# The linear half of an expert's first bias taken off TensorE: ScalarE copies the product out, GpSimd adds the bias

## What is computed

```python
def expert_block(args):
    xblk, e = args                      # 128 rows of one expert
    hh = xblk @ w1[e] + b1[e]           # 1024 -> 2048
    glu = jnp.minimum(hh[:, :D_FF], SWIGLU_LIMIT)
    lin = jnp.clip(hh[:, D_FF:], -SWIGLU_LIMIT, SWIGLU_LIMIT)
    act = glu * jax.nn.sigmoid(SWIGLU_ALPHA * glu) * (lin + 1.0)
    return act @ w2[e] + b2[e]
```

## Time and profile before

| | us |
|---|---|
| median of three runs | 2271.59 (2271.05 to 2272.78) |
| the profiled execution | 2271.8 |
| its span, first to last instruction | 2269.9 |
| TensorE busy in the span | 2235.8 |
| VectorE, ScalarE, GpSimd busy | 1768.0, 1238.6, 429.3 |
| start of item 0 to end of the last | about 1087 to 2260 |

### The profile page before, as it was taken

One profiled execution on the slowest core, in us unless ns is written; L12 is line 12 of the kernel. 1 busy time (PEld: TensorE's weight loads), 2 busy tenths in 40 slices (PEclk: granted clock), 3 DMA queues, 4 the chain that ended last, 5 costly groups with the idle time before them and its releaser, 6 DMA issues.

```text
span 2269.9 us, 30685 instructions
## 1 busy us (share of the span) xinstructions
PE 2235.8 (98%) x10681; PEld 1828.9 (81%) x10681; DVE 1768.0 (78%) x1652; ACT 1238.6 (55%) x1154; POOL 429.3 (19%) x421
## 2 busy tenths in 40 slices
PE   7999999999999999999999999999999999999998
PEld 3888888888887887888788888888888888888886
DVE  6756655555646766757899999999999999999997
ACT  6322132222225624632777777777777777777774
POOL 3000000000221132102522222222212222223222
PEclk9999999999999999999999999999999999999999
DMA  8322223131321121146899999999999999999995
GB/s 301 121 93 93 98 88 130 56 130 57 105 98 38 38 75 38 57 149 215 310 360 367 374 373 375 386 367 371 381 362 372 370 369 383 370 376 372 385 365 199
DMA packets 135516, 542.98 MB, mean 239 GB/s; under 512 B 16131, under 2 KB 24467, under 8 KB 101390
## 3 DMA queue, kind: packets, MB, share of 16 engines
q1 hardware_dynamic: 123192, 516.30, 60.1%
q0 software_dynamic: 11952, 21.44, 3.9%
q10 hardware_dynamic: 296, 4.21, 0.5%
HBM read 533.79 MB, written 26.38 MB: 247 GB/s over the span
## 4 chain that ended last, share of the span: by engine, by line
PE 95%; DMA 2%; DVE 1%; POOL 1%; ACT 0%; issue 0%; SPq 0%; POOLq 0%; DVEq 0%
PE ps L2272 90%; PE ps L2828 1%; PE ps L2840 1%; PE ps L2619 1%; POOL list_d L865 1%; DMA ar<-h_d,ar 0%; DMA ar<-in_ctx 0%; PE ps L2564 0%; DMA out_x<-ar,cur 0%; DMA raw<-in_w_mod 0%; PE ps L2510 0%; PE ps L2384 0%; DVE nmx L1875 0%; ACT hhi L1026 0%; PE ps L2717 0%
## 5 line engine op out<-in xcount | busy, mean ns | idle before, releaser
L2272 PE MATMUL ps<-whi,yhi 128*128 128x512 f32 x1072 | 346.5, 393 | 0.1
L2272 PE MATMUL ps<-hhi,yhi 128*128 128x512 f32 x1072 | 342.6, 389 | 0.0
L2092 DVE TENSOR_TENSOR hlo<-raw,hhi 128x2048 fp32r<-128x2048 f32 x132 | 302.6, 2294 | 47.3 <-ACT hhi L1333 47.3
L1333 ACT ACTIVATE whi<-raw 128x2048 fp32r<-128x2048 f32 x132 | 253.5, 1921 | 98.9 <-PE ps L2272 98.9
L2092 DVE TENSOR_TENSOR wlo<-raw,whi 128x2048 fp32r<-128x2048 f32 x132 | 298.7, 2282 | 3.4 <-ACT whi L1333 1.9
L1333 ACT ACTIVATE hhi<-raw 128x2048 fp32r<-128x2048 f32 x132 | 253.1, 1918 | 76.5 <-PE ps L2272 76.5
L1450 DVE TENSOR_TENSOR wlo<-raw,whi 128x2048 fp32r<-128x2048 f32 x56 | 128.2, 2289 | 159.5 <-ACT whi L995 159.4
L2272 PEld LDWEIGHTS ps<-whi,yhi 128*128 128x128 f32 x1072 | 201.2, 188 | 53.9 <-issue 12.1
L2272 PEld LDWEIGHTS ps<-hhi,yhi 128*128 128x128 f32 x1072 | 201.2, 188 | 41.7
L2272 PE MATMUL ps<-whi,hhi 128*128 128x512 f32 x592 | 233.3, 394 | 0.0
L2272 PE MATMUL ps<-whi,hlo 128*128 128x512 f32 x592 | 230.8, 390 | 0.0
(11 more groups left out here) (355 smaller groups left out, 4436.6 us busy)
## 6 DMA issues: line engine op xcount, KB each, us to landing
raw<-in_exp_w SPq DMA_DIRECT2D x264, 1024.0 KB, 7.7
ar<-in_exp_w SPq DMA_DIRECT2D x132, 1024.0 KB, 7.6
raw<-in_w_in SPq DMA_DIRECT2D x44, 1024.0 KB, 5.0
raw<-in_w_mod SPq DMA_DIRECT2D x22, 1024.0 KB, 6.4
raw<-in_w_br_ret SPq DMA_DIRECT2D x8, 1024.0 KB, 5.0
ar<-in_x SPq DMA_DIRECT2D x8, 512.0 KB, 7.4
raw<-in_w_br_diff SPq DMA_DIRECT2D x4, 1024.0 KB, 5.1
raw<-in_w_out SPq DMA_DIRECT2D x4, 1024.0 KB, 9.6
```

Of the source, the lines that this page charges most:

```text
L1333: act.activation(e_whi[j % ESPL], e_raw[s], ACT.Copy).then_inc(e_hi, 1)
L2092: V.tensor_tensor(e_wlo[j % ESPL], e_raw[s], e_whi[j % ESPL].bitcast(F32), ALU.subtract).then_inc(e_lo, 1)
L2272: return pe.matmul(out, lhsT, rhs, start=start, stop=stop, skip_group_check=skip)
```

## The change

- TensorE adds the bias of the gated half alone: two matmuls for four. The table `bias` shrinks to 512 columns with the gated half's first 512 columns in rows 0 to 63 and its second 512 in rows 64 to 127; banks 4 and 5 now begin with their first product.
- Before the stage, ScalarE adds the 1 to the linear half of b1 and stores it (two DMAs from its own queue) in a scratch tensor in DRAM, `acc_d`.
- SP loads, for each item, the row of its expert from there, broadcast to 128 partitions (128 x 1024, `load_linear_bias`, into `A_LIN`), between the loads of w1 and w2.
- ScalarE copies the linear half out of PSUM (`linear_out`) into `A_AC`; it makes the last chunk's high part before it and takes the Silu only after `x_high`.
- GpSimd adds `A_LIN` to `A_AC` (`add_linear_bias`). For this its order changes: column, add and gather stand ahead of the wait for the landing.
- VectorE clips in place in SBUF, after the last chunk's split and `x_low`.

```diff
-        bias = [hh[0][:, 2, q, :] for q in range(2)]
+        bias = hh[0][:, 2, 0, :]
...
+            def load_linear_bias(e, i):
+
+                if not isinstance(i, int):
+                    sp.wait_ge(moe_step, i * 3)
+                sp.dma_start(F(A_LIN, D), acc_d[one(e), :].broadcast_to((P, D))).then_inc(b_loaded, 16)
...
+            sp.wait_ge(stored, 16 * (LT + 2))
+            load_linear_bias(0, 0)
             with sp.Fori(1, N_EXPERTS) as i:
                 for j in range(FIRST):
                     load_w1(i, i, j)
+                load_linear_bias(i, i)
                 for k in range(MOE_N - FIRST):
                     load_w2(i - 1, i, FIRST + k, k)
...
+            def add_linear_bias(i):
+
+                pool.wait_ge(b_loaded, i * 16 + 16 * (BIASES + 1))
+                pool.wait_ge(moe_step, i * 3 + 1)
+                hold()
+                pool.tensor_tensor(out=F(A_AC, D), in0=F(A_AC, D), in1=F(A_LIN, D), op=ALU.add).then_inc(moe_step, 1)
...
+                next_sel(i, e1)
+                add_linear_bias(i)
+                next_gather(i, code2, i * 4 + 1)
                 if not isinstance(k, int) or k:
                     take_rows(k)
-                next_sel(i, e1)
-                next_gather(i, code2, i * 4 + 1)
+                    pool.wait_ge(cur_ready, k + 1)
+                    hold()
...
             next_sel(0, 1)
+            add_linear_bias(0)
             next_gather(0, 2, 1)
...
+            def linear_out(i):
+                act.wait_ge(e_used, chunk(i, FIRST - 1) + 1)
+                act.activation(F(A_AC, D), psf[:, 4 * COL:6 * COL], ACT.Copy).then_inc(moe_step, 1)
...
+                hi_e(i, MOE_N - 1)
+                linear_out(i)
+                x_high(i + 1)
                 glu(i)
-                hi_e(i, MOE_N - 1)
-                x_high(i + 1)
...
+            act.activation(linear, linear, ACT.Identity, bias=ones[0:2 * N_EXPERTS, 0:1]).then_inc(bias_hi, 1)
+            act.activation(bias, F(A_BSRC, COL), ACT.Copy).then_inc(bias_hi, 1)
             act.wait_ge(bias_hi, 1)
-            for q in range(2):
-                act.activation(bias[q], bsrc[:, q * COL:(q + 1) * COL], ACT.Copy).then_inc(bias_hi, 1)
+            for r in range(2):
+                act.dma_start(acc_d[0:N_EXPERTS, r * COL:(r + 1) * COL],
+                              linear[32 * r:32 * r + 32, :]).then_inc(stored, 16)
...
-            def activate(i, between):
-
-                dve.wait_ge(e_used, chunk(i, FIRST - 1) + 1)
-                V.tensor_scalar(ac, psf[:, 4 * COL:6 * COL], 1.0 - LIMIT, 1.0 + LIMIT, ALU.max,
-                                ALU.min).then_inc(moe_step, 1)
-                between()
+            def activate(i):
+
+                dve.wait_ge(moe_step, i * 3 + 2)
+                V.tensor_scalar(ac, ac, 1.0 - LIMIT, 1.0 + LIMIT, ALU.max, ALU.min).then_inc(moe_step, 1)
                 dve.wait_ge(glu_done, i + 1)
-                dve.wait_ge(moe_step, i + 1)
+                dve.wait_ge(moe_step, i * 3 + 3)
...
-                activate(i, lambda: lo_e(i, MOE_N - 1))
+                lo_e(i, MOE_N - 1)
                 x_low(i + 1)
+                activate(i)
...
-                    for b in (0, 2, 1, 3):
-                        r = slice(b // 2 * 64, b // 2 * 64 + 64)
-                        last = mm(ps[:, 2 + b, :], sel[r, :], bias[b % 2][r], not late, False)
+                    for b in range(2):
+                        r = slice(b * 64, b * 64 + 64)
+                        last = mm(ps[:, 2 + b, :], sel[r, :], bias[r], not late, False)
...
-                        mm(o, xthi[:, kk, :], wh, late and kk == 0, False)
+                        mm(o, xthi[:, kk, :], wh, kk == 0 and (late or b > 1), False)
```

More of the change, by code:

```diff
@@ L137 @@
 A_XG, A_Y, A_GS, A_TH, A_AC = 0, 1024, 2048, 3072, 9216
+A_LIN, A_LSRC = A_TH, A_BSRC + COL
+BIASES = 6
 MOD_A = 2 * D // COL
@@ L696, in _ @@
             for r in range(4):
-                sp.dma_start(F(A_BSRC, D)[32 * r:32 * r + 32, :], a["exp_b1"][:, r // 2 * D:(r // 2 + 1) * D]).then_inc(b_loaded, 16)
+                sp.dma_start(F(A_BSRC, COL)[32 * r:32 * r + 32, :],
+                             a["exp_b1"][:, r // 2 * COL:(r // 2 + 1) * COL]).then_inc(b_loaded, 16)
+            for r in range(2):
+                sp.dma_start(F(A_LSRC, COL)[32 * r:32 * r + 32, :],
+                             a["exp_b1"][:, D + r * COL:D + (r + 1) * COL]).then_inc(b_loaded, 16)
             def one(e):
@@ L749, in extra @@
                     load_w1(e, i, j)
+                load_linear_bias(e, i)
                 for k in range(MOE_N - FIRST):
@@ L762, in _ @@
             sp.wait_ge(last_added, 32)
-            sp.wait_ge(stored, 16 * LT)
+            sp.wait_ge(stored, 16 * (LT + 2))
         @block.gpsimd
@@ L956, in _ @@
             next_sel(0, 1)
+            add_linear_bias(0)
             next_gather(0, 2, 1)
             pool.sem_inc(pool_m, 3)
-            pool.wait_ge(stored, 16 * LT)
+            pool.wait_ge(stored, 16 * (LT + 2))
             for t in range(LT):
@@ L1385, in _ @@
             hi_e(0, 1)
-            act.wait_ge(b_loaded, 64)
-            bsrc = F(A_BSRC, D)
-            act.activation(bsrc[64:128, :], bsrc[64:128, :], ACT.Identity, bias=ones[64:128, 0:1]).then_inc(bias_hi, 1)
+            act.wait_ge(b_loaded, 16 * BIASES)
+            linear = F(A_LSRC, COL)[0:2 * N_EXPERTS, :]
+            act.activation(linear, linear, ACT.Identity, bias=ones[0:2 * N_EXPERTS, 0:1]).then_inc(bias_hi, 1)
+            act.activation(bias, F(A_BSRC, COL), ACT.Copy).then_inc(bias_hi, 1)
             act.wait_ge(bias_hi, 1)
-            for q in range(2):
-                act.activation(bias[q], bsrc[:, q * COL:(q + 1) * COL], ACT.Copy).then_inc(bias_hi, 1)
+            for r in range(2):
+                act.dma_start(acc_d[0:N_EXPERTS, r * COL:(r + 1) * COL],
+                              linear[32 * r:32 * r + 32, :]).then_inc(stored, 16)
             hi_e(0, 2)
@@ L1403, in bias_out @@
                 if t == 0:
-                    act.wait_ge(stored, 16 * LT)
+                    act.wait_ge(stored, 16 * (LT + 2))
                 act.wait_ge(gb_done, t + 1)
@@ L1418, in _ @@
             act.activation(junk32[:, 0:1], ones[:, 0:1], ACT.Silu)
+            linear_out(0)
             glu(0)
@@ L2227, in _ @@
             dve.wait_ge(ones_made, 5)
[L2228 to L2232, removed]
+            dve.wait_ge(bias_hi, 2)
+            V.scalar_tensor_tensor(out=bias, in0=bias.bitcast(F32), scalar=low_rows[:, 0:1],
+                                   in1=F(A_BSRC, COL), op0=ALU.mult, op1=ALU.add).then_inc(bias_lo, 1)
             dve.wait_ge(gb_hi, 2)
@@ L2241, in _ @@
                 lo_e(1, j)
-            activate(0, lambda: None)
+            activate(0)
             x_low(1)
@@ L2861, in up @@
                         pe.wait_ge(xt_lo, 2)
-                        pe.wait_ge(bias_lo, 2)
+                        pe.wait_ge(bias_lo, 1)
                         add_bias()
```

## The result

The changed kernel takes **2284.66 us** (median; 2283.33 to 2286.35), the kernel before 2271.65 (2271.05 to 2272.78) in the same runs: ratio 1.0059, 95% interval 1.0047 to 1.0070. It is 13.0 us slower, outside the range of the forecast. Its profiled execution took 2283.33 us, span 2281.5.

A forecast was written before the change was run, and what follows sets the result against it. TensorE was taken as the bound, busy for 98% of the span. Terms of -7.4 us (bias matmuls) and +4.8 us (start), the others 0, summed to -2.6 us: 2269.0 us predicted, range for 8 in 10 from 2264 to 2282.

The forecast's parts named there:

- The pair of bias matmuls: TensorE, each item: two bias matmuls fewer save 0.23 us, over 32 items -7.4 us (-4.8 to -10.7).
- The longer chain: Behind each item, through ScalarE, GpSimd's add and VectorE's clip: next split 0.9 us later, within spare time, 0 us.
- The third rival: Small stalls in some items, about 0.3 us on average, turn -2.6 into +7: 2279 us; chance 0.08.
- More DMA: One more 0.52 MB broadcast per item, queued on SP between w1 and w2, fits the DMA stream: 0 us.
- Rival 1: Broadcast has no room in the DMA stream: 1.40 us per item, +48 us, 2320; full form or part, chance 0.11.
- The start: Start of expert stage: item 0's add, queued behind GpSimd's list wait, delays item 1's bias matmuls, +4.8 us (+3.5 to +7).

The follow-up runs named there:

- the small load: The changed kernel, but after item 0 the transfer of the linear bias carries 32 of its 1,024 columns, GpSimd still adding all 1,024: 2275.2 us.

## Why the prediction was wrong, point by point

- **The pair of bias matmuls: right.** 35.07 us between undisturbed turns, 0.23 less, as forecast.
- **The longer chain: the times right, the zero wrong.** The product was forecast at 1607.7, 7.4 us behind the turn, and stands at 7.5. The hold-up by VectorE's split came as argued (the addition needs 2.35 us free, not 2.07; the clip 0.69, not 0.81). This zero is the second step that failed: it had been argued for items without a late load. The chain took 2.2 of the 5.2 us of room that the product had before (5.3 to 10.5), and an item that follows a late load needs that room: 12.8 us between the addition on GpSimd and on VectorE, some 6 of them in the start, the rest in stalls. The third rival, small stalls of 0.3 us on average at a chance of 0.08, had the size of the stalls right: 10.2 us over 31 items is 0.33. Its 2279 us falls short for want of the end.
- **"More DMA", 0 us: the step that failed.** The prediction took 391 GB/s of one item and 426 of nine microseconds as what the stream can do, and read 3.8 us to spare out of a load's landing. Those rates were bursts. And the item of 356 GB/s that it took for an ordinary one lies low: it stands right behind an item with a scatter, and of the 31 items of before only two move less (346 and 350); the mean is 373. So the need after the change is 13.7 MB an item, not 13.1, against the 13.8 that the forecast itself allowed. The kernel with two unused loads shows 390 GB/s over 1000 us with TensorE waiting for it. At 390, an item of before had 35.30 - 13.17/0.390 = 1.5 us of stream to spare (373 x 35.30 = 13.17 MB). The change adds 0.52 MB and takes 0.23 us away: 13.70/0.390 = 35.1 us for a turn of 35.07. By that mean nothing is left; by the 398 GB/s of the undisturbed items it would be 0.6 us. Either way what a bias-row scatter puts into the queue is worked off slowly or not at all: ScalarE's copy stays late from item 8 to the last, and with the small load it recovers. That the stream's level is the reason is worked out from these rates, not tested by itself. The price is 9.5 us in the changed kernel (2284.7 - 2275.2), 7.2 where VectorE adds. Rival 1, at 0.11, was the right mechanism in "a part of it"; its full form, 48 us, assumed 373 as the limit. The Trainium skill's figure of about 358 GB/s for loads from HBM ("SBUF — State Buffer", "Summary: rules for kernel authors") is under what was sustained here: 388 GB/s over 1000 us without a wait of TensorE in the kernel before with one unused load.
- **The start: the mechanism right, the number in part by luck.** +4.8 forecast, +5.2 read; with the 0.23 us that the pair saves in this item taken out, 5.4 for this term. The mechanism is in the rows (GpSimd, VectorE, TensorE; the last one is the stretch behind TensorE's wait, columns as in the earlier trace rows), and moving the addition ahead gave 3.7 us back:

```profile
1117.20 2.35 POOL L923 TENSOR_TENSOR ar<-ar 128x1024 f32<-128x1024 f32 x1
...
1119.58 0.69 DVE L2222 TENSOR_SCALAR ar<-ar 128x1024 f32<-128x1024 f32 x1 [8.21 <-POOL ar L923]
...
1121.66 1.77 PE L2872 MATMUL ps<-cst,ar 128*128 128x128 f32 x8 [3.12 <-DVE ar L2225]
...
1121.91:1125.33 3.42, 3.42 (x13) 2.46 (x12) 3.42 (x4) 1.20 (x2) 1.34 (x2) 0.50 0.48 174
```

  TensorE waits 3.12 us for the product, and right behind that wait the granted clock is 0.50, the lower level, for 3.4 us: the eight transposes take 1.77 us, not the 1.04 of before, where the clock stayed at 1.00. I put this at about 1.4 us: x_low is done at 1122.80, so the bias matmuls, which start at 1123.36, could have started 0.56 us sooner, and the item takes 0.8 us longer from there to its turn (1146.54 - 1123.36 = 23.18, against 1141.37 - 1118.76 - 0.23 = 22.38). The forecast had no such term. Without it the start would have cost about 4.0 us, less than the 4.8 because GpSimd made the column 1.0 us sooner than before (1116.94, before 1117.94). In four other profiles with that addition behind the list the turn comes 4.2 to 7.9 us late, so +7 as the upper bound was a little low; in the two latest of them, 7.1 and 7.9, the lower clock lasts 6.8 us and not 3.4.

- **The end: not priced at all.** Whatever is late when the last item comes shows behind it: +3.2 us in the changed kernel (the last turn of activations waits 1.82 us for the product, a matmul behind it 1.16 us for VectorE), +2.8 where VectorE adds with the whole load, +0.8 with half of it. That the two go with the same lateness is read from the profiles; no run took it apart.

Open: why the turn of the activations behind item 0 starts anywhere from 1120.5 to 1123.4 us in the five profiles with the same code there; why the lower clock lasts 3.4 us in three of them and 6.8 in two (these two things make up the 3.7 us between their starts); and whether the shorter turn or VectorE's fuller queue makes the transfer dear.

## What to carry to other kernels

Read a stream's limit from a stretch in which the bound engine waits for it, or push it there with loads that nobody reads; bursts, the time to landing and an engine's waits for loads did not show it here. Before giving work to an idle engine, ask for the bytes it brings and for the room that it takes from the chain after a disturbance, not in the regular item, and don't price the two apart: here 6.5 and 6.7 us alone were 16.2 together. When a period gets shorter, every stream that was almost full becomes fuller by itself.

## What the hardware showed that I had not expected

- The core's 16 DMA engines gave 390 GB/s over 1000 us of these loads at a share of 1.00, and 398 over 176 us of them at 1.01, though nearly the same share (0.99 and 1.02) was read at 373 and 426 GB/s in the kernel before: the share does not tell how full the stream is.
- VectorE's operation on two SBUF tensors and GpSimd's on SBUF exclude each other in both directions, and the wait is recorded within the later one's duration: additions of 2.35 us read as 3.51, one of 0.24 as 1.35, a split of 2.29 as 3.99. The Trainium skill says that they exclude each other ("SBUF — State Buffer", "Who interferes with whom"); the traces agree.
- After waits of 0.26, 1.30 and 1.04 us in the worst item, and after the one of 3.12 us in the start, TensorE's clock was granted at 0.50, its lower level, for 3.4 us (two matmuls in 1.06 us instead of 0.62): a wait can cost more than its own length.
